# State space stage divided anew over the engines, at the head of a four-layer kernel on one core

## What is computed

```python
def s5_mixer(x, a_re, a_im, log_dt, b_re, b_im, c_re, c_im, d_skip, w_glu, w_out):
    u = x.reshape(bsz, seq, 64, 16)
    dt = exp(log_dt)[:, None]
    lbar = exp(min(a_re, -1e-4) * dt) * (cos(a_im * dt) + i sin(a_im * dt))
    coef = (lbar - 1) / lam
    bb = coef[..., None] * (b_re + i b_im)
    bu = einsum('blgh,gph->lbgp', u, bb)
    s = associative_scan(s[t] = lbar * s[t-1] + bu[t])      # over 256 tokens
    y = Re(einsum('lbgp,ghp->blgh', s, c_re + i c_im)) + d_skip * x
    h = gelu(y)
    val, gate = split(h @ w_glu, 2)
    return (val * sigmoid(gate)) @ w_out
```

## Time and profile before

| | us |
|---|---|
| median of 3 runs | 1463.2 (1461.89 to 1465.09) |
| the profiled execution | 1462.21 |
| its span in the profile | 1460.4 |
| TensorE busy (share of the span) | 1383.9 (95%) |
| VectorE | 958.0 (66%) |
| ScalarE | 689.7 (47%) |
| GpSimd | 10.1 (1%) |
| first instruction of gelu in the state space stage | 115.53 |
| the 32 DMA issues for `toep` | 73.71 to 102.57 |
| the scan on VectorE | 85.27 to 108.02 |

### The profile page before, as it was taken

How to read it: one execution, slowest core, us unless ns; L and a number is a source line. 1 busy time by engine, 2 the same in 40 slices (tenths; PEclk the granted TensorE clock), 3 DMA queues, 4 the chain that set the end, 5 groups by cost and what they waited for, 6 DMA issues and landing times.

```text
span 1460.4 us, 27765 instructions
## 1 busy us (share of the span) xinstructions
PE 1383.9 (95%) x11695; PEld 1342.4 (92%) x11695; DVE 958.0 (66%) x1255; ACT 689.7 (47%) x853; POOL 10.1 (1%) x8
## 2 busy tenths in 40 slices
PE   5759999999999999999989999999999999999998
PEld 4548999999988899999979998999999999899998
DVE  7996687555664587555787567765447756777542
ACT  4746463343565363343556454444344644444432
POOL 0100000000000000000000000000000000000000
PEclk7779999999999999999999999999999999999999
DMA  5078557676452457666444354557665435465761
GB/s 127 1 109 218 177 142 202 181 191 175 145 171 90 116 143 203 176 190 182 145 145 121 111 173 153 194 176 198 174 182 165 125 107 174 145 200 173 195 180 58
DMA packets 340448, 227.54 MB, mean 156 GB/s; under 512 B 21672, under 2 KB 335248, under 8 KB 340128
## 3 DMA queue, kind: packets, MB, share of 16 engines
q1 hardware_dynamic: 340352, 226.14, 54.2%
HBM read 222.70 MB, written 1.05 MB: 153 GB/s over the span
## 4 chain that ended last, share of the span: by engine, by line
PE 72%; DVE 12%; ACT 9%; issue 3%; SPq 2%; DMA 1%; ACTq 0%; DVEq 0%
PE PS L400 22%; PE PS L402 21%; PE PS L401 21%; DVE w_lo L381 5%; ACT w_hi L376 4%; SPq L1430 1%; PE PS L1163 1%; ACT res L815 1%; PE PS L1482 1%; DMA x_chunk<-in_x_dram 1%; PE PS L1498 1%; DVE raw_lo L980 1%; DVE sqr L987 1%; ACT x_group L1595 0%; PE PS L1463 0%
## 5 line engine op out<-in xcount | busy, mean ns | idle before, releaser
L381 DVE TENSOR_TENSOR w_lo<-raw,w_hi 128x2048 fp32r<-128x2048 f32 x208 | 475.8, 2291 | 210.0 <-ACT w_hi L376 209.9
L400 PE MATMUL PS<-x_hi,w_hi 128*128 128x256 f32 x1824 | 522.2, 286 | 8.1 <-DVE w_lo L381 7.0
L401 PE MATMUL PS<-x_lo,w_hi 128*128 128x256 f32 x1824 | 517.2, 284 | 0.0
L402 PE MATMUL PS<-x_hi,w_lo 128*128 128x256 f32 x1824 | 517.1, 283 | 0.0
L376 ACT ACTIVATE w_hi<-raw 128x2048 fp32r<-128x2048 f32 x208 | 397.1, 1910 | 230.6 <-PE PS L402 227.8
L400 PEld LDWEIGHTS PS<-x_hi,w_hi 128*128 128x128 f32 x1824 | 350.9, 192 | 12.5 <-DVE w_lo L381 8.0
L400 PE MATMUL PS<-hid_hi,w_hi 128*128 128x256 f32 x1248 | 354.5, 284 | 6.6 <-DVE hid_lo L664 6.6
L401 PE MATMUL PS<-hid_lo,w_hi 128*128 128x256 f32 x1248 | 353.1, 283 | 0.0
L402 PE MATMUL PS<-hid_hi,w_lo 128*128 128x256 f32 x1248 | 353.1, 283 | 0.0
L401 PEld LDWEIGHTS PS<-x_lo,w_hi 128*128 128x128 f32 x1824 | 351.2, 193 | 0.1
L402 PEld LDWEIGHTS PS<-x_hi,w_lo 128*128 128x128 f32 x1824 | 350.9, 192 | 0.0
(11 more groups left out here) (363 smaller groups left out, 1377.3 us busy)
## 6 DMA issues: line engine op xcount, KB each, us to landing
raw<-in_w_ff_dram SPq DMA_DIRECT2D x128, 512.0 KB, 4.5
raw<-in_ffn_w_gu_dram SPq DMA_DIRECT2D x88, 512.0 KB, 5.2
raw<-in_w_in_dram SPq DMA_DIRECT2D x68, 512.0 KB, 4.8
raw<-in_sb_w_qkv_dram SPq DMA_DIRECT2D x24, 512.0 KB, 4.5
raw<-in_ffn_w_down_dram SPq DMA_DIRECT2D x20, 512.0 KB, 4.6
raw<-in_ssm_w_glu_dram SPq DMA_DIRECT2D x16, 512.0 KB, 6.4
raw<-in_w_out_dram SPq DMA_DIRECT2D x16, 512.0 KB, 4.5
raw<-in_ssm_w_out_dram SPq DMA_DIRECT2D x8, 512.0 KB, 4.5
```

The source lines that it names most:

```text
L381: nc.vector.tensor_tensor(w_lo[s][:, :], raw[s][:, :], w_hi[s][:, :].bitcast(F32), ALU.subtract).then_inc(lo_done, 1)
L400: nc.tensor.matmul(dst, lhs_hi, r_hi, start=start, stop=False, skip_group_check=True)
L401: nc.tensor.matmul(dst, lhs_hi, r_lo, start=False, stop=False, skip_group_check=True)
L402: return nc.tensor.matmul(dst, lhs_lo, r_hi, start=False, stop=stop, skip_group_check=True)
```

## The change

All of it is in the state space stage, with the same mathematics in another order.

- **Toeplitz.** `kernels` now multiplies the lag tables (from the input tables) with `tab_c[0]`, 16 columns a group: the result is the *last* 16 columns of `toep` for all 8 row blocks. d is added by a multiplication with the constant `last_rows`. The other columns are this one moved up by 16 rows: `shifted` moves it by one, two or three blocks of rows with a multiplication by a shifted identity, 32 groups at a time, and `s5_moves` copies the lower right quarter to the upper left with one DMA for each half of the groups. The 32 DMAs and `kern` are gone. Zeroes come by DMA from a constant.
- **Input tables.** `tab_b[1]` isn't computed any more; TensorE swaps the halves of `tab_b` (constant `swap`) into PSUM, one quarter is copied to `b_swap`.
- **Division.** GpSimd computes the coefficients, half of `x_group`, lag block 3, the diagonal of d, and the output tables of blocks 0 to 2 (for block 2 the second product stays apart in `s_more`, and TensorE adds it by 16 more multiplications with the states). VectorE keeps lag blocks 0 to 2 and output block 3, and reads powers, swapped table and scratch from PSUM, where ScalarE has copied the powers (`powers`) and the scan's factors (`carries`).
- **Chunk inputs.** `chunk_inputs` multiplies the other way round (weights `s_in`), so that the result needs no second turning. TensorE's steps and ScalarE's evictions are one list of items (`ITEMS`), over three PSUM banks; block order 0, 1, 3, 2.
- **Loads.** b before c, three loads each instead of four; log_dt and a_im are issued by ScalarE. x by token is a load of its own (`x_tok`), turned behind the multiplications with `toep`.
- **Weight chunks.** Chunk 0 waits for the lags, chunk 1 for the output tables.

```diff
+            if isinstance(j, int) and j == 0:
+                eng.wait_ge(lag_done, NB - 1)
+                eng.wait_ge(lag_added, 1)
+                eng.wait_ge(lag_tail, NB)
+            elif isinstance(j, int) and j == 1:
+                eng.wait_ge(sout_pool, NB - 1)
+                eng.wait_ge(sout_dve, 1)
+                eng.wait_ge(item_ready, ITEM["k2"] + 1)
+            elif isinstance(j, int) and j == 2:
                 eng.wait_ge(intra_done, 1)
...
-        def s5_toeplitz(sp):
-
-            sp.wait_ge(toep_zero, 1)
-            for b in range(NB):
-                sp.wait_ge(k_done, 4 * b + 4)
-                for t in range(SL):
-                    sp.dma_start(toep[SH * t:SH * t + SH, BQ * b:BQ * b + BQ, SH * t:P],
-                                 kern[32 * b:32 * b + SH, :, 0:P - SH * t]).then_inc(k_moved, 16)
+        def s5_moves(sp):
+
+            for half in range(2):
+                sp.wait_ge(item_taken, ITEM[f"s{half}3"] + 1)
+                gs = halves_of_groups(half)
+                sp.dma_start(toep[0:SP, gs, 0:SP], toep[SP:P, gs, SP:P]).then_inc(toep_moved[half], 16)
...
+            a = CONST["right"][0]
+            sp.dma_start(toep[SP:P, :, 0:SP], w["consts"][SP:P, a:a + SP].unsqueeze(1).to_broadcast([SP, SG, SP])).then_inc(toep_zero, 16)
+            sp.wait_ge(item_ready, ITEM["d2"] + 1)
+            sp.dma_start(x_tok[:, :, :], w["x"][0].rearrange("(a p) d -> p a d", p=P)).then_inc(ld_tok, 16)
...
+            def turned_lags(b):
+                if b == 3:
+                    pe.wait_ge(lag_added, 1)
+                else:
+                    pe.wait_ge(lag_done, b + 1)
+                pe.wait_ge(lag_tail, NB)
+                for q in range(4):
+                    bank = begin(f"t{b}{q}")
+                    for i in range(4):
+                        last = nc.tensor.transpose(PS[:, bank, P * i:P * i + P],
+                                                   lag[b][:, 4 * q + i, :, :].rearrange("p t h -> p (t h)"), ident)
+                    last.then_inc(item_ready, 1)
+
+            def chunk_inputs(b):
+                taken(f"t{b}3")
+                taken("u3")
+                bank = begin(f"d{b}")
+                for j in range(BQ):
+                    last = nc.tensor.matmul(PS[:, bank, SC * j:SC * j + SC], s_in[:, j, :], u_in[:, BQ * b + j, :],
+                                            start=j == 0, stop=True, skip_group_check=True)
+                last.then_inc(item_ready, 1)
+
+            def kernels(b):
+                pe.wait_ge(tabs_done, 2)
+                pe.wait_ge(diag_done, 1)
+                pe.wait_ge(ld_const, 32)
+                bank = begin(f"k{b}")
+                for j in range(BQ):
+                    nc.tensor.matmul(PS[:, bank, SH * j:SH * j + SH], lag[b][:, j, :, :].rearrange("p t h -> p (t h)"),
+                                     tab_c[0][:, BQ * b + j, :], start=j == 0, stop=False, skip_group_check=True)
+                a = CONST["last_rows"][0]
+                nc.tensor.matmul(PS[:, bank, 0:SH * BQ], const[0:SH, a:a + P],
+                                 d_diag[:, BQ * b:BQ * b + BQ, :].rearrange("h g k -> h (g k)"), start=False, stop=True,
+                                 skip_group_check=True).then_inc(item_ready, 1)
+
+            def shifted(half, k):
+                bank = begin(f"s{half}{k}")
+                nc.tensor.matmul(PS[:, bank, :].rearrange("p (g h) -> p g h", h=SH), shift_to(k),
+                                 toep[:, halves_of_groups(half), P - SH:P], start=True, stop=True).then_inc(item_ready, 1)
...
+            def inputs_by_state(b):
+                take(f"d{b}")
                 for two in range(2):
                     for ri in range(2):
...
+                        if b == 2 and ri == 1:
+                            continue
+                        if b == 2 and two == 1:
+                            act.wait_ge(din_dve, 2)
+                        last = nc.scalar.activation(*input_places(b, two, ri), ACT.Copy)
+                last.then_inc(item_taken, 1)
...
+            def carries():
+                act.wait_ge(sout_first, 1)
+                for half in range(2):
+                    ps = slice(SP * half, SP * half + SP)
+                    rows = PS[ps, 2, 0:2 * SG].rearrange("p (e g) -> p e g", e=4)
+                    re = pow_t[ps, 0, SL, :].rearrange("p (g two) -> p two g", two=2)[:, half, :]
+                    im = pow_t[ps, 1, SL, :].rearrange("p (g two) -> p two g", two=2)[:, half, :]
+                    sign = -1.0 if half else 1.0
+                    nc.scalar.activation(rows[:, 0, :], re, ACT.Copy)
+                    nc.scalar.activation(rows[:, 3, :], re, ACT.Copy)
+                    nc.scalar.activation(rows[:, 1, :], im, ACT.Copy, scale=sign)
+                    nc.scalar.activation(rows[:, 2, :], im, ACT.Copy, scale=-sign).then_inc(carry_done, 1)
...
+            state_set(0, 16)
+            act.wait_ge(sout_pool, NB - 1)
+            for r in range(4):
+                act.wait_ge(xt_ready, r + 1)
+                nc.scalar.activation(res[:, 2 * r:2 * r + 2, :].rearrange("p a t -> p (a t)"), PS[:, res_bank(r), :],
+                                     ACT.Copy).then_inc(xt_done, 1)
+            state_set(16, 8)
+            state_set(24, 8)
...
+                o_x, o_y = (pow_t[:, i, 1:SL + 1, gs].rearrange("p t g -> p g t").unsqueeze(3).to_broadcast(sh) for i in range(2))
+                Q.tensor_tensor(s_out[:, gs, :, :], tab_c[0][:, gs, :].unsqueeze(2).to_broadcast(sh), o_x,
+                                ALU.mult).then_inc(pool_step, 1)
+                step.one()
+                y_table = tab_c[1][:, gs, :].unsqueeze(2).to_broadcast(sh)
+                if b == 2:
+                    pool.wait_ge(item_ready, ITEM["k2"] + 1)
+                    Q.tensor_tensor(s_more[:, :, :, :], y_table, o_y, ALU.mult).then_inc(sout_pool, 1)
+                    continue
+                Q.tensor_tensor(tmp[:, :].rearrange("p (g t h) -> p g t h", g=BQ, h=SH), y_table, o_y, ALU.mult).then_inc(pool_step, 1)
+                pool.wait_ge(pool_step, step.one())
+                so = s_out[:, gs, :, :].rearrange("p g t h -> p (g t h)")
+                Q.tensor_tensor(so, so, tmp[:, :], ALU.add).then_inc(sout_pool, 1)
...
+            pow_x = PS[:, 2, :].rearrange("p (k g) -> p k g", g=SG)
+            pow_y = PS[:, 3, :].rearrange("p (k g) -> p k g", g=SG)
+            part = PS[:, 0:2, :].rearrange("p a b -> p (a b)")
+            HQ = BQ // 2
+            dve.wait_ge(pow_copied, 1)
+            for b in range(3):
+                gs = slice(BQ * b, BQ * b + BQ)
+                sh = [P, BQ, SL - 1, SH]
+                V.tensor_tensor(lag[b][:, :, 0:SL - 1, :], tab_b[:, gs, :].unsqueeze(2).to_broadcast(sh),
+                                pow_x[:, SL - 2::-1, gs].rearrange("p t g -> p g t").unsqueeze(3).to_broadcast(sh),
+                                ALU.mult).then_inc(dve_step, 1)
+                v_count.one()
+                if b == 0:
+                    dve.wait_ge(swap_ready, 2)
+                elif b == 2:
+                    dve.wait_ge(swap_done, 1)
+                sh = [P, HQ, SL - 1, SH]
+                tv = part[:, 0:HQ * (SL - 1) * SH].rearrange("p (g t h) -> p g t h", g=HQ, h=SH)
+                for h in range(2):
+                    g0 = BQ * b + HQ * h
+                    gs = slice(g0, g0 + HQ)
+                    swapped = PS[:, 3 + 4 * (g0 // 32), SH * (g0 % 32):SH * (g0 % 32) + SH * HQ].rearrange("p (g h) -> p g h", h=SH)
+                    V.tensor_tensor(tv, swapped.unsqueeze(2).to_broadcast(sh),
+                                    pow_t[:, 1, SL - 1:0:-1, gs].rearrange("p t g -> p g t").unsqueeze(3).to_broadcast(sh),
+                                    ALU.mult).then_inc(dve_step, 1)
+                    dve.wait_ge(dve_step, v_count.one())
+                    la = lag[b][:, HQ * h:HQ * h + HQ, 0:SL - 1, :]
+                    V.tensor_tensor(la, la, tv, ALU.add).then_inc(lag_done if h else dve_step, 1)
+                    dve.wait_ge(lag_done if h else dve_step, b + 1 if h else v_count.one())
+
+            gs = slice(3 * BQ, 4 * BQ)
+            sh = [P, BQ, SL, SH]
+            dve.wait_ge(item_ready, ITEM["u3"] + 1)
```

More of the change, by code:

```diff
@@ L1521, in s5_tensor @@
[L1521 to L1530 removed]
+            pe.wait_ge(ld_swap, 16)
+            pe.wait_ge(tabb_done, 1)
+            for h in range(2):
+                nc.tensor.matmul(PS[:, 3 + 4 * h, :], C("swap"), tab_b[:, halves_of_groups(h), :].rearrange("p g h -> p (g h)"),
+                                 start=True, stop=True).then_inc(swap_ready, 1)
@@ new lines, in s5_tensor @@
+            turned_lags(0)
+            chunk_inputs(0)
+            turned_lags(1)
+            chunk_inputs(1)
+            turned_lags(3)
+            chunk_inputs(3)
+            turned_lags(2)
+            chunk_inputs(2)
+            kernels(0)
+            kernels(1)
+            taken("k1")
```

(31 more changed lines are left out.)

605 lines of the change are left out of this document (276 added, 329 removed).

## The result

The change made the kernel slower: 1488.1 us in the median of four runs (1487.6 to 1490.5) against 1462.7 for the kernel before on the same chip. The ratio is 1.0174, with a 95% interval of 1.0156 to 1.0192. The forecast was 1445.7, so the change cost 25.4 us where 17.5 were to be gained.

The account below looks back on a forecast made before the run. Before gelu, DMA issues, VectorE and TensorE ended within some 5 us; then the block loop would bind. Gelu at 98.0 against 115.5 saves 17.5: 1462.2 - 17.5 = 1444.7, 1445.7 for the median; 8-in-10 range 1438 to 1455.

Parts of the forecast that it names:

- the block loop on TensorE becomes the bound: Turned lags, products and spreading run serially, 7.9 us taken per block; scan starts at 64.7 instead of 85.3.
- The second copy of the table: Toeplitz stage: second DMA copying half the table down 64 partitions, 3 to 8 us, taken as 5.3.
- C: Beside GpSimd's work every VectorE instruction is held, PSUM-fed or not; gelu at 129.2, 1477 us; chance 0.06.
- B: VectorE instructions reading only SBUF are held, the scan's reduction too; scan ends near 99, 1453.3 us; chance 0.09.
- D: GpSimd slower on four-dimensional patterns, above 5.5 us an instruction its tables end late; 1463 us at 7.1; chance 0.05.
- four products of 16 groups: Toeplitz stage on TensorE: replace the 64 kernel products, 2.3 us each with the diagonal.
- the clock from before: Block loop on TensorE: granted clock 0.78 on the mean, about half of the time at either level.
- Rival A: Clock stays at 1.2 GHz through the block loop, blocks of 8.9 us, gelu at 103; 1450.7 us; chance 0.18.
- the six shifts: Toeplitz stage on TensorE: six shifts of 512 columns that move the last columns up, 0.95 us each.
- waits between them: Toeplitz stage: waits for evictions around the products and shifts, 1.6 us.
- last shift's copy to the last state copy: Tail: table copy 5.3 us, second half of `toep` products 1.8, x transposes 2.1, late state copies until 92.4.
- from there to the gelu: Tail: two weight splits of 1.91 us and 1.33 to gelu, 0.4 for the clock, state products (4.6) beside the splits.

Follow-up runs that it names:

- kernel with both stages turned round: Changed kernel with chunk inputs and kernels multiplied with narrow weights in four column tiles, then turned back, and input spreading put behind the next block's turned lags: 1441.7 us.
- the loop's serial order kept: Changed kernel with chunk inputs and kernels both turned round, each block's spreading still in front of the next block's turned lags: 1450.2 us.
- kernel with only its kernels turned round: Changed kernel with only the kernels (last Toeplitz columns) reversed: table C as 32-column weights in four column tiles, lags moving, then turned back: 1468.9 us.

## Why the prediction was wrong, step by step

**What held.** That the block loop on TensorE becomes the bound, the plan of time up to it, and single terms behind it. `x` was there at 18.1 (forecast 18.3), VectorE began the lags at 20.85 (21.5), the input turns ended at 31.7 (32.3), the lags' sum at 42.1 (43), with instructions of 2.02 and 1.09 us (2.03 and 1.1). The second copy of the table took 5.2 (5.3). The scan kept its step. Behind the gelu nothing changed.

**The rivals.** C, every VectorE instruction held by GpSimd, did not occur: the lag instructions kept their time beside GpSimd's of 3.4 to 4.5. (The terms of its scan start add to 97.5, not to 99.5.) B, the scan's reduction held because it reads only SBUF, could not occur in the changed kernel, since GpSimd was done with all but one table at 63.6 and the scan ran from 79.09 to 101.82. The kernel with both stages turned round shows it: there the scan began beside GpSimd, and its reductions took what they take alone (timelines of GpSimd and VectorE):

```profile
55.76 4.54 POOL L1903 TENSOR_TENSOR s_out<-s_out,tmp 128x2048 f32<-128x2048 f32 x1
...
59.08 0.38 DVE L2041 TENSOR_REDUCE run<-terms 128x64 f32<-128x192 f32 x1 [0.16 <-DVE terms L2039]
```

Up to 64.2, the end of GpSimd's next table, the steps stayed at 0.73. The port rule of the Trainium skill (SBUF — State Buffer, SBUF: two separate sides) is what the traces show for large instructions with one operand in PSUM and for this reduction. D did not occur either: GpSimd's large instructions took 3.4 to 4.5. Its last product, forecast for 72 to 82, came at 111.78, as it waits for TensorE's kernels; the path did not wait for it. That the kernel got slower was given 0.07, nearly all of it for C, and it came by none of the paths that I had priced.

**The step that failed** is in the block loop: "TensorE multiplies (32 passes with 128 weight columns: 0.055 us each at 2.4 GHz, half of the 0.109 that L1463 took at 1.2 GHz, so 1.8 or 3.5)", and with the same price the "four products of 16 groups (2.3 each with the diagonal)". L1463 is a transposition. The nearest row by tile shape was not the nearest by kind of instruction. A pass of a product with 128 weight columns costs twice as much, 0.115 and 0.220, at either clock.

**The second error** was to take the clock from before, half of the time at either level, for a stage whose instructions were changed. Rival A had the low clock, and it came true in the loop and beyond it. Its 1450.7 was computed with the wrong price and let the clock rise again soon behind the loop, which is why even the rival lay 37 us off.

The 43.6 us between the forecast gelu (98.0) and the one measured (141.6) are then all accounted for:

| stretch | forecast | measured | difference |
|---|---|---|---|
| start of the first kernels: 1.1 in the first block, 8.7 in two that took 12.2 instead of 7.9, 4.2 in the last | 62.8 | 76.8 | 14.0 |
| the four kernels with diagonals | 9.2 | 25.5 + 4.9 | 21.2 |
| the six shifts | 5.7 | 4.7 + 5.5 | 4.5 |
| waits between them | 1.6 | 1.0 | -0.6 |
| last shift's copy to the last state copy (table, second half, x by token, at a low clock) | 13.1 | 14.6 | 1.5 |
| from there to the gelu | 5.6 | 8.7 | 3.1 |

The sum is 43.7. The first two rows are the price of the passes and the low clock together, some 4.5 us for each of the eight groups of passes over what I had taken for them. In the second row the two can be told apart: at the high clock a block costs 3.65 and its diagonal 0.69 by the rows above, 17.4 for four, so 8.2 of the 21.2 is the price and 13.0 the clock. The shifts, the diagonals and, in the main, the fifth row are the clock. The last row is a cover that was gone: I had put the state products beside two splits of weights, but they took from 133.0 to 141.0 (the timeline's 2.28 of ScalarE waiting for L1604), since 32 passes were added and the clock began at 0.50.

**What the removed part was worth.** In the kernel with both stages turned round, the other parts of the change are as they were, and it gains 21.3 us over the one before, against a forecast of 17.5. So the DMA issues, the loads, the tables on GpSimd and what else was moved together bring somewhat more than was expected; with the loop's serial order kept, as the forecast had it, the gain is 12.7 (1450.2). The orientation of two multiplications, with the serial order of the loop that came with it, gave 46 us away. How the 21.3 divide among those parts was not tried.

**A rule that spoke against the change.** The kernel before multiplied the chunk inputs in four column tiles with 32 weight columns, 1.08 us for 32 passes at the high clock (L1506 in its trace, at 48.38), and the change gave this up to save the turning back. The Trainium skill (TensorEngine Tiling (Array Packing), When to Use Tiling) advises just this swap with column tiles where the moving side has 64 columns or fewer. The runs agree, 7.03 to 1.93 at the same granted clock. I had read the change as the removal of turns, and never priced what it removed on the multiplication's side.

## What to carry to other kernels

Count the weight columns of a product, not its moving ones: a f32 product with 128 weight columns cost 0.44 us at the low clock with 16, 32 or 64 moving columns, so put the narrow operand into the array, in four column tiles, and pay for turning back (in one column tile alone the 32 passes took 5.88, not 1.93). Take the price of an operation from a row of the same kind, a product from a product, and where the trace has none, let the range hold twice the price. When a stage's instructions on TensorE change, its granted clock is an unknown of its own; here it was worth as much as the whole change.

## What the runs showed of the hardware that I had not expected

- A record of a f32 product with 128 weight columns took 0.22 us at a granted 0.50, with 32, 64 or 128 rows and 32 moving columns, and with 16 or 64 moving columns and 128 rows; at 1.00 it took 0.115 with 32 and 0.117 with 128 moving columns. With 64 weight columns it took 0.113, a transposition with 128 weight columns and 32 moving 0.113, both at 0.50.
- With TensorE busy for 35.2 of 36 us by these passes and the shifts, the granted clock was 0.55. With the same passes and 128 moving columns it was 1.00 in the same stage. During a fill of 512-column products it rose to 0.99, and behind the 32 passes that followed it was soon at 0.50 again in three blocks of four. What decides it stays open.
- The same kernel's time hangs on the clock that an execution gets: six runs of one kernel lay between 1446.9 and 1456.2, with mean granted clocks from 0.991 to 0.978. The identical passes of the first block took 4.11 in the profiled execution of the changed kernel and 7.03 in that of the kernel with only its kernels turned round.
- GpSimd's products of 1792 and 2048 f32 elements a partition took 3.4 and 3.85, its additions 4.0 and 4.5; VectorE's with one operand in PSUM were not slowed beside them, nor was its reduction of the scan, which reads only SBUF (0.38).
